# Two attention key heads scored on the two halves of the tensor array, and the last key block of a unit kept in plain fp32

## What is computed

```python
q, k, v, f = jnp.split(x @ w_in, ...)            # 8 x 64 | 2 x 64 | 2 x 64 | 4 x 128
logits = q_blk . k_blk * scale + bias            # k_blk: up to 3 blocks of 128 keys
m = max(max(logits), sink);  p = exp(logits - m)
probs = p / (sum(p) + exp(sink - m))
out = probs . v_blk
mix = concat(rms_norm(attn), rms_norm(four)) @ w_o
x = LN(alpha*x + mix);  x = LN(alpha*x + ConvFFN(x))
```

## Time and profile before

| | us |
|---|---|
| median of 3 runs | 1004.63 |
| the profiled execution's own time | 1004.8 |
| its span, first to last instruction | 1003.0 |
| PE busy | 984.0 (98%) |
| DVE busy | 734.7 (73%) |
| ACT busy | 465.0 (46%) |
| POOL busy | 220.2 (22%) |

### The profile page before, as it was taken

The page is one execution under the profiler, slowest core; times in us unless marked ns, Lnnn a source line. Parts: engine busy times, 40 slices in busy tenths (PEclk is TensorE's granted clock), DMA queues, the critical chain, the costliest instruction groups (busy, mean ns, idle before and its releaser), DMA issues.

```text
span 1003.0 us, 12249 instructions
## 1 busy us (share of the span) xinstructions
PE 984.0 (98%) x4588; PEld 819.9 (82%) x4588; DVE 734.7 (73%) x1110; ACT 465.0 (46%) x742; POOL 220.2 (22%) x210
## 2 busy tenths in 40 slices
PE   5999999999999999999999999999999999999997
PEld 4888888998888788888888888888888888888885
DVE  6665566886786799778788778778777394665587
ACT  5574666896413754544554454554457402113000
POOL 2300426775850000000000000000000299500022
PEclk9999999999999999999999999999999999999999
DMA  8335141008240223222222322322339522414022
GB/s 306 97 66 166 35 114 43 1 1 245 92 147 22 84 64 97 80 76 84 84 85 72 96 85 65 104 85 63 105 130 353 210 69 99 167 40 171 0 84 84
DMA packets 91179, 102.11 MB, mean 102 GB/s; under 512 B 20091, under 2 KB 71247, under 8 KB 91120
## 3 DMA queue, kind: packets, MB, share of 16 engines
q1 hardware_dynamic: 89904, 99.15, 29.9%
q10 hardware_dynamic: 1216, 2.17, 0.7%
HBM read 79.29 MB, written 22.02 MB: 101 GB/s over the span
## 4 chain that ended last, share of the span: by engine, by line
PE 92%; DVE 5%; issue 1%; ACT 1%; DMA 1%; POOL 0%; SPq 0%; DVEq 0%; ACTq 0%
PE ps L698 30%; PE ps L699 30%; PE ps L700 30%; PE ps L906 1%; PE ps L1035 1%; DVE g_lo L1165 1%; DVE prob L1367 1%; DVE d_lo L1165 1%; DVE pTl L1165 1%; DMA acc<-in_x_prompt 1%; ACT prob L1898 1%; DVE bn L1168 1%; PE ps L727 1%; DVE part_sum L1677 0%; ACT pTh L1721 0%
## 5 line engine op out<-in xcount | busy, mean ns | idle before, releaser
L698 PE MATMUL ps<-d_hi,g_hi 128*128 128x512 f32 x352 | 137.0, 389 | 0.1
L699 PE MATMUL ps<-d_lo,g_hi 128*128 128x512 f32 x352 | 136.9, 389 | 0.0
L700 PE MATMUL ps<-d_hi,g_lo 128*128 128x512 f32 x352 | 136.9, 389 | 0.0
L665 POOL TENSOR_TENSOR acc<-acc,gain_bc 128x1024 f32<-128x1024 f32 x12 | 32.8, 2730 | 466.5 <-ACT bias_bc L1721 466.5
L698 PEld LDWEIGHTS ps<-d_hi,g_hi 128*128 128x128 f32 x352 | 66.1, 188 | 14.3 <-DVE d_lo L1165 0.5
L700 PEld LDWEIGHTS ps<-d_hi,g_lo 128*128 128x128 f32 x352 | 66.1, 188 | 13.8
L699 PEld LDWEIGHTS ps<-d_lo,g_hi 128*128 128x128 f32 x352 | 66.1, 188 | 13.5
L698 PE MATMUL ps<-x1h,wa_hi 128*128 128x512 f32 x192 | 75.6, 394 | 0.0
L700 PE MATMUL ps<-x1h,w_lo 128*128 128x512 f32 x192 | 74.8, 389 | 0.0
L699 PE MATMUL ps<-x1l,wa_hi 128*128 128x512 f32 x192 | 74.7, 389 | 0.0
L2018 ACT ACTIVATE hc<-U,taps 128x512 f32<-128x512 f32 x60 | 48.7, 813 | 44.8 <-DVE U L1546 41.4
(11 more groups left out here) (296 smaller groups left out, 2732.1 us busy)
## 6 DMA issues: line engine op xcount, KB each, us to landing
w_raw<-in_w_up SPq DMA_DIRECT2D x44, 512.0 KB, 4.9
g_scratch<-gated SPq DMA_DIRECT2D x22, 512.0 KB, 2.6
g_raw<-g_scratch SPq DMA_DIRECT2D x22, 512.0 KB, 6.2
d_raw<-in_w_down SPq DMA_DIRECT2D x22, 512.0 KB, 7.3
acc<-in_x_sample SPq DMA_DIRECT2D x8, 512.0 KB, 12.5
st_raw<-in_w_in SPq DMA_DIRECT2D x16, 256.0 KB
x_scratch<-acc SPq DMA_DIRECT2D x8, 512.0 KB, 3.5
acc<-x_scratch SPq DMA_DIRECT2D x8, 512.0 KB, 8.0
```

The source lines that it names most:

```text
L665: chain.mark(pool.tensor_tensor(dst, dst, gain_bc[:], ALU.mult))
L698: pe.matmul(out, whi, xhi, start=start, stop=False, skip_group_check=onto)
L699: pe.matmul(out, whi, xlo, start=False, stop=False, skip_group_check=onto)
L700: return pe.matmul(out, wlo, xhi, start=False, stop=stop, skip_group_check=onto)
```

## The change

The two key heads are no longer padded to 128 rows: `kh` and `kl` are one tile of 128 rows x 512 keys (head 0 in rows 0 to 63, head 1 in rows 64 to 127), and a score's products run on its 64 rows alone. Scores are issued in pairs, one of key head 0 and one of key head 1 (heads j = 2, 3 of unit n + 2 with heads j = 0, 1 of unit n + 3), and their three products alternate. The last key block of each unit is not split: it is copied once from PSUM into `pTw` (fp32), by DVE in units of three key blocks and by ACT in units of two, and weighed by one plain fp32 matmul with an unsplit V, `vzf`. Further: `PAIRS` puts three blocks of sequence 0 first; `prob` and its sums have four slots; K's parts take one copy and one subtraction per sequence instead of two of each; the zeroing of K is gone (8 memsets); V is copied once more on DVE (4 instructions) and one more memset per sequence is on POOL; the transposes of a unit's first two blocks stand together. The SBUF addresses of the projection and attention tiles are laid out anew (not shown), with their loads at the same places of the queues.

```diff
-PAIRS = ((0, 0), (1, 0), (0, 1), (1, 1), (2, 0), (2, 1), (3, 0), (3, 1))
+PAIRS = ((0, 0), (1, 0), (2, 0), (0, 1), (1, 1), (2, 1), (3, 0), (3, 1))
...
+def score_pairs(n):
+    return [[(m, j) for m, j in ((n + 2, 2 + half), (n + 3, half)) if 0 <= m < UNITS] for half in range(2)]
+SCORES = [s for n in range(-3, UNITS - 2) for pair in score_pairs(n) for s in pair]
+def score_count(m, j):
+    return SCORES.index((m, j)) + 1
...
+def weigh_kind(n, i):
+    blocks = len(key_blocks(unit(n)[0]))
+    return "parts" if i < blocks - 1 else "whole_dve" if blocks == 3 else "whole_act"
+def blocks_of(kinds, n, i=0):
+    return sum(weigh_kind(v, j) in kinds for v in range(min(n + 1, UNITS)) for j in range(len(key_blocks(unit(v)[0]))) if v < n or j < i)
+BY_ACT, BY_DVE = ("parts", "whole_act"), ("parts", "whole_dve")
...
-            def scores(n, j):
-                blk, b, kv = unit(n)
-                kbs = key_blocks(blk)
-                s = GRP * n + j
-                keys = slice(kbs[0] * P, (kbs[-1] + 1) * P)
-                if j == 0:
-                    if n == 0:
+            def scores(pair):
+
+                for m, j in pair:
+                    if (m, j) == (0, 0):
                         pe.wait_ge(f_lo, 16)
-                        pe.wait_ge(qk_lo, 6)
-                        pe.wait_ge(kz_zero, 4)
-                    elif n == 4:
-                        pe.wait_ge(qk_lo, 12)
-                        pe.wait_ge(kz_zero, 8)
-                if s >= 3:
-                    pe.wait_ge(logit_done, s - 2)
-                mm3(ps[:, s % 3, 0:len(kbs) * P], qh[b][:, j, blk * P:(blk + 1) * P], ql[b][:, j, blk * P:(blk + 1) * P],
-                    kh[b][:, kv, keys], kl[b][:, kv, keys], True, True).then_inc(s_ps, 1)
+                        pe.wait_ge(qk_lo, 5)
+                    elif (m, j) == (6, 0):
+                        pe.wait_ge(qk_lo, 10)
+                    if score_count(m, j) > 3:
+                        pe.wait_ge(logit_done, score_count(m, j) - 3)
+                for step in range(3):
+                    for m, j in pair:
+                        blk, b, kv = unit(m)
+                        kbs = key_blocks(blk)
+                        rows, tok, keys = slice(kv * HD, (kv + 1) * HD), slice(blk * P, (blk + 1) * P), slice(kbs[0] * P, (kbs[-1] + 1) * P)
+                        q, k = (ql if step == 2 else qh)[b][rows, j, tok], (kl if step == 1 else kh)[b][rows, keys]
+                        last = pe.matmul(ps[:, (score_count(m, j) - 1) % 3, 0:len(kbs) * P], q, k, start=step == 0, stop=step == 2)
+                        if step == 2:
+                            last.then_inc(s_ps, 1)
...
-                if n:
-                    pe.wait_ge(pt_lo, min(pt_before(n - 1) + i + 1, pt_before(n)))
+                held = [v for v in range(n) if i < len(key_blocks(unit(v)[0]))]
+                if held:
+
+                    m = held[-1]
+                    if weigh_kind(m, i) == "whole_act":
+                        pe.wait_ge(pt_hi, blocks_of(BY_ACT, m, i + 1))
+                    else:
+                        pe.wait_ge(pt_lo, blocks_of(BY_DVE, m, i + 1))
                 if n == 2 and i == 2:
-                    pe.wait_ge(qk_lo, 12)
...
+                    if weigh_kind(n, i) != "parts":
+                        last = pe.matmul(ps[:, 6 + e % 2, :], vzf[b][:, kb, kv * HD:kv * HD + P], pTw[:, n % 2, :],
+                                         start=kv == 0 and i == 0, stop=kv == 1 and i == len(kbs) - 1)
+                        continue
...
-            for j in range(3):
-                scores(0, j)
+            for pair in score_pairs(-3):
+                scores(pair)
             project(10, 0)
-            scores(0, 3)
-            scores(1, 0)
-            scores(1, 1)
+            scores(score_pairs(-2)[0])
             project(10, 1)
-            scores(1, 2)
-            scores(1, 3)
+            scores(score_pairs(-2)[1])
             project(11, 0)
+            scores(score_pairs(-1)[0])
             four_square_sums()
+            scores(score_pairs(-1)[1])
 
             for n in range(UNITS):
                 if n == 1:
                     project(11, 1)
                 if n >= UNITS - 2:
                     out_four(n - UNITS + 2)
-                for j in range(GRP):
-                    if n + 2 < UNITS:
-                        scores(n + 2, j)
-                    if 1 <= j <= len(key_blocks(unit(n)[0])):
-                        turn_probs(n, j - 1)
+                first, second = score_pairs(n)
+                scores(first)
+                turn_probs(n, 0)
+                turn_probs(n, 1)
+                scores(second)
+                if len(key_blocks(unit(n)[0])) == 3:
+                    turn_probs(n, 2)
...
-                for kv in range(KV):
-                    rows = slice((1 - kv) * HD, (2 - kv) * HD)
-                    dve.memset(f32(kh[b][rows, kv, :]), 0.0).then_inc(kz_zero, 1)
-                    dve.memset(f32(kl[b][rows, kv, :]), 0.0).then_inc(kz_zero, 1)
-
             def proj_low(j):
                 b, i = divmod(j, TILES)
                 dve.wait_ge(qk_hi, qk_count(j))
                 if i == KTILE:
-                    for kv in range(KV):
-                        rows = slice(kv * HD, (kv + 1) * HD)
-                        lo_part(kl[b][rows, kv, :], ps[rows, 4 + j % 2, :], kh[b][rows, kv, :], qk_lo)
+                    lo_part(kl[b][:], ps[:, 4 + j % 2, :], kh[b][:], qk_lo)
...
+                    dve.tensor_scalar(vzf[b][:, :, cols], vps[:, :, kv * HD:(kv + 1) * HD], 1.0, None, ALU.mult).then_inc(vz_lo, 1)
...
-                dve.wait_ge(pt_hi, pt_before(n) + i + 1)
+                if weigh_kind(n, i) == "whole_act":
+                    return
+                if weigh_kind(n, i) == "whole_dve":
+                    dve.wait_ge(pt_ps, pt_before(n) + i + 1)
+                    if n >= 2:
+                        dve.wait_ge(pv_done, n - 1)
+                    dve.tensor_scalar(pTw[:, n % 2, :], ps[:, 3 + i, :], 1.0, None, ALU.mult).then_inc(pt_lo, 1)
+                    return
+                dve.wait_ge(pt_hi, blocks_of(BY_ACT, n, i + 1))
                 lo_part(pTl[:, n % 2, i, :], ps[:, 3 + i, :], pTh[:, n % 2, i, :], pt_lo)
...
+                first, second = score_pairs(n)
+                if n == 0:
+                    for s in score_pairs(-1)[1]:
+                        logits(*s)
+                for s in first:
+                    logits(*s)
+                if n >= 4 and n % 2 == 0:
+                    attn_low(n // 2 - 2)
+                if n - 1 in WO_UNITS:
+                    wo_low(0, WO_UNITS.index(n - 1))
+                probs_low(n, 0)
+                for s in second[0:1]:
+                    logits(*s)
+                probs_low(n, 1)
+                for s in second[1:2]:
+                    logits(*s)
+                if len(key_blocks(unit(n)[0])) == 3:
+                    probs_low(n, 2)
...
+                if weigh_kind(n, i) == "whole_act":
+                    copy(pTw[:, n % 2, :], ps[:, 3 + i, :], pt_hi)
+                else:
+                    copy(pTh[:, n % 2, i, :], ps[:, 3 + i, :], pt_hi)
...
+                for s in first[0:1]:
+                    exp(*s)
+                probs_high(n, 0)
+                for s in first[1:2]:
+                    exp(*s)
+                probs_high(n, 1)
+                for s in second[0:1]:
+                    exp(*s)
+                if len(key_blocks(unit(n)[0])) == 3:
+                    probs_high(n, 2)
+                for s in second[1:2]:
+                    exp(*s)
```

More of the change, by code:

```diff
@@ L178, in build @@
     nsink8 = keep("nsink8", [P, HEADS])
[L179 to L181 removed]
+    negm = keep("negm", [P, 4, GRP])
+    rowsum = keep("rowsum", [P, 4, GRP])
+    rden = keep("rden", [P, 4, GRP])
     vf = keep("vf", [P, TT])
@@ L627, in _ @@
             pool.wait_ge(s1_ps, NSEQ * FG)
-            for n in range(3):
+            for n in range(4):
                 set_sink(n)
@@ L1388, in _ @@
             dve.wait_ge(sink_ready, 1)
-            for j in range(GRP):
-                logits(0, j)
+            logits(0, 0)
+            logits(0, 1)
             st_low(11)
+            logits(0, 2)
             logits(1, 0)
+            proj_low(10)
+            logits(0, 3)
             logits(1, 1)
-            proj_low(10)
             logits(1, 2)
-            logits(1, 3)
-            zero_keys(1)
+            logits(2, 0)
             dve.wait_ge(ssf_ps, 1)
@@ L1402, in _ @@
                     proj_low(11)
-                for j in range(GRP):
-                    if n + 2 < UNITS:
-                        logits(n + 2, j)
-                    if j == 1 and n >= 4 and n % 2 == 0:
-                        attn_low(n // 2 - 2)
-                    if j == 1 and n - 1 in WO_UNITS:
-                        wo_low(0, WO_UNITS.index(n - 1))
-                    if 1 <= j <= len(key_blocks(unit(n)[0])):
-                        probs_low(n, j - 1)
```

(27 more changed lines are left out.)

227 lines of the change are left out of this document (117 added, 110 removed).

## The result

The changed kernel takes 1008.5 us (median of 6 runs, 1007.56 to 1009.11) against 1004.82 us of the kernel before beside it (6 runs, 1004.22 to 1005.79): ratio 1.0037, 95% interval 1.0027 to 1.0046. It is slower by 3.7 us, where 4.8 less had been forecast. 1008.5 lies just inside the range, on the wrong side of no change. The profiled execution has a span of 1005.8 us and a time of its own of 1007.56, the lowest of the six; in the traces the difference is 2.8 us.

What follows compares the result with a forecast made beforehand. PE was taken as the bound, busy 984.0 of 1003.0 us. Terms -12.6 + 3.3 + 3.7 + 0.8 = -4.8 us against 1004.8 gave 1000.0, stated as 999.8 for the median; range 995 to 1009.

Steps and rivals of the forecast that it cites:

- Scores in pairs: Score products on PE: the two halves work at once, the narrower product of each pair costs nothing; 12.6 us less.
- Rivals 1 (loading): Score pairs: loads of both halves queue up, only 7.4 us saved; 1004.2 us, chance 0.15.
- 3 (no overlap): The six products of each of 30 pairs: halves don't overlap, so nothing is hidden; 1011.6 us, chance 0.20.
- Entering and leaving the half array: Around score calls on PE: 66 changes of shape, 27 already paid, 39 at 0.085; 3.3 us more.
- the upper bound of 8.3: Changes of shape: each costs a product's whole tail, 66 x 0.16 less 27 x 0.085; 8.3 us more.
- Rival 2: Changes of shape around score calls: each empties the array, 0.16 us each; 1004.0 us, chance 0.13.
- The last block in plain fp32: Weighing on PE: 16 plain products at 0.92 us replace three products of 0.23 each; 3.7 us more.
- DVE and ACT in the loops: Attention loops: PE stays longest, but the DVE and ACT chain costs 0.1 us on each of eight loops; 0.8 us lost.
- rival 4: Attention loops: the DVE and ACT chain rules, waits of 4 us instead of 0.8; 1003.0 us, chance 0.07.
- First loops: Units 0 and 1: last scores move, yet nothing waits for POOL's normalising; margin below 1 us.
- Costs nothing: Beside PE's gapless projections: removed memsets and K splits, four V copies and POOL's memset change no time.

Runs made afterwards that it cites:

- joined: The kernel before, with PE transposing all blocks of a unit together behind the second score; 1004.48 us, ratio 0.9999.
- no_plain: The changed kernel with the last key block split and weighed in three products as before, no plain fp32 product; 1007.15 us, ratio 1.0026.
- early_parts: The changed kernel without the plain fp32 product and with the square sums moved behind the first half of projection 10; 1006.43 us, ratio 1.0017.
- one_pass: The changed kernel with `pTw` and `vzf` as fp32r, so the last block takes one pass and its low parts are left out; 1002.03 us, ratio 0.9971.
- early_one_pass: The changed kernel with the last block in one fp32r pass and the square sums behind the first half of projection 10; 1000.67 us, ratio 0.9962.
- sums_early: The changed kernel with the square sums moved from just before the loops to behind the first half of projection 10; 1006.88 us, ratio 1.0021.
- half_before: The kernel before, with each score's products on the 64 rows of its own key head, order unchanged; 1022.04 us, ratio 1.0167.
- full_rows: The changed kernel with each score product on all 128 rows, so each score sums both key heads; 1007.2 us, ratio 1.0028.
- full_one_pass: The kernel before, all 128 rows, with each unit's last key block weighed by one fp32r product of the high parts; 1000.17 us, ratio 0.9955.

## Why the prediction was wrong

*Scores in pairs*, -12.6: right. The distance between the products of a pair and the next is that of one product, for both widths, and loads of both halves coincide. Rivals 1 (loading) and 3 (no overlap) are out. The Trainium skill, "TensorE: Matmul & The Clock Gate", Part 3, says about 4 ns between starts; the trace agrees, with mostly 3 to 10 ns in pairs of equal width.

*Entering and leaving the half array*, +3.3: **this is the step that failed**, by 7.3 us, more than the whole forecast gain. Three things were wrong in it. The price was taken from the nearest row, a change of format at 0.085; `joined` shows that this row holds no change of anything. So the 27 changes that were to be free because a format change was already paid weren't free. And the upper bound of 8.3 subtracted the same 27; without that subtraction it would have been 10.6, which is what was measured: 64 changes (not 66; the last pair ahead of the loops and the first loop's first pair adjoin, which I had overlooked) at 0.166. The tail of a product, 0.39 - 0.23 = 0.16, gives the right size, and it stood in the text as a bound; that a change waits for just this tail is not shown. Rival 2 had the price right, and the timelines bear out its mechanism, a gap on each side of a stretch on halves; only its time, 1004.0, carried the same subtraction (without it, 1006.3); it had been argued down with the row that was misread.

*The last block in plain fp32*, +3.7: right in kind (four passes), off in size. 0.86 and not 0.92, so 2.7. Four passes of one instruction run a little quicker than four fp32r products.

*DVE and ACT in the loops*, +0.8: about right for the kernel after, 0.8 us more of waits than before, though 0.5 of them lie in the first loop. What had been put as rival 4 is nonetheless there, covered by PE's extra 10.6: with PE's list shortened the waits for logits are 2.8 (`no_plain`), 3.5 (`early_parts`), 4.7 (`one_pass`) and 5.2 us (`early_one_pass`). This is why taking work off PE's list returned only half to two thirds of it.

*First loops*, nothing waits: wrong. The first pair of the first loop waits 0.51 us (160.81), and not for POOL, which the prediction had looked at, but for DVE to read the logits of the pairs just ahead. The square sums now stand between scores on halves. Behind them the clock fell for 3.4 us. That 1.7 us had no term at all in the sum.

*Costs nothing:* right, 100 to 150 us and all behind the attention are unchanged.

The sum with the measured terms is -12.6 + 64 x 0.166 + 2.7 + 1.7 + 0.8 = 3.2 against 3.2 in the stretch. The 0.166 is worked out from this very stretch, so that the sum closes is no proof; the proof is that two others, `sums_early` (0.17) and `half_before` (0.16 overall, 0.177 in a loop), give nearly the same.

Open: what brings the clock down. It fell behind sums and half-array pairs with a short wait (after), with PE busy all the time (`half_before`), already from 150 us on in `early_parts`, and stayed up in the profiled executions of `sums_early`, `full_rows` and `early_one_pass`. It also differs between executions of one kernel (`half_before`, `early_parts`, `one_pass`), so a single trace says little of it. No experiment took sums, halves and waits apart one by one. Open too is why the price of a change spreads from 0.16 to 0.185. A part is seen in the loop of `half_before`: leaving the half for transposes and coming back costs 0.10 ahead of them, 0.23 in them and 0.02 behind, 0.17 for each of the two changes; coming to the half from a product of 512 columns costs 0.10 ahead of the first product and 0.10 behind it, 0.20.

## What to carry to other kernels

Two products on the two halves of the array cost as much as one, but each change between a half and the whole array cost 0.16 to 0.20 us here: a stretch of pairs pays only from what it hides beyond two changes, some 0.35 us, and a pair of 3 x 256 columns hides just that. An offset seen behind a block of instructions is a switching cost only if it stays the same when the block gets longer; try that before it prices anything, and before it excuses other changes from theirs. And before PE's list is shortened, look at how late the next engine is: here a third to a half of what was further taken from PE's list turned into waits for DVE's logits. And read the cost of a wait from the distances of starts: the list of waits showed only about half of a short one.

## What was not expected of the hardware

- The two halves don't keep to each other's order: with three products of one half listed ahead of three of the other, the starts are the same to 0.01 us, and in a pair of unequal widths each half keeps its own pace.
- A change between 64 and 128 rows costs 0.16 to 0.20 us, spread over both sides of it; a change between fp32r products and fp32 transposes costs nothing that could be measured.
- An fp32 transpose of 128 columns takes 0.11 us, a plain fp32 product of 512 columns 0.86.
- The granted clock was 0.60 over 5 us in which PE was busy for all 5.00, behind 5 us of the same at 0.72 (`half_before`, 160 to 170 us).
- A wait of PE that the list of waits gives as 0.33 us cost 0.60 in distances of starts (`full_one_pass`, 191.31 to 192.26 us).
